# Gate and up projections by two levels of seven products, their outer weight sums made earlier and kept in DRAM

## The chip, the cores and the metric

One core of one Trainium2 chip runs the whole program. The metric is the device time of one execution in microseconds (us). Engines: TensorE (PE, its weight loads PEld), VectorE (DVE), ScalarE (ACT), GpSimd (POOL), and the queue that issues all DMAs here (SP).

## The reference

Two blocks over 512 latent tokens (and 256 context tokens in the first), width 1024, all float32: an attention and mLSTM layer, a gated linear attention layer, and then a second block with an RG-LRU branch, a gated delta branch, a merge, and a feed-forward part. The change touches the feed-forward part:

```python
    h = rmsnorm(x, ffn_norm[l])
    gu = h @ w_gate_up[l]            # 512 x 1024 by 1024 x 5632
    gt, up = jnp.split(gu, 2, axis=-1)
    x = x + (jax.nn.silu(gt) * up) @ w_down[l]
```

and, for where the new sums are made, the RG-LRU branch (12 blocks of 128 channels: a convolution over time, four 128x128 gate products, a scan forward and one backward).

## The kernel before

Data is held transposed, 128 channels by 512 tokens to a tile. One list, ORDER, holds steps such as ("gu", 3); each engine runs the steps that it knows in the order of that list (three engines take some steps of the delta stage a few places later) and waits on semaphores, so the list sets the order of work on every queue. Weights stream from DRAM into a ring of three places of 4096 columns (`ring`); SP goes through the same list, issues a place's next load once the step that frees it is passed, and waits in order for what each DMA needs.

**Gate and up.** D_FF is 2816, which makes 22 pairs j of 128 gate and 128 up columns. Pair 0 is computed plainly (32 matmul instructions of 512 columns, L1929; a float32 product is two instructions). Pairs 1 to 21 use Winograd's form of Strassen: the 2x2 blocks are the halves of the inner dimension, gate against up, and the halves of the tokens. Seven products of 4 inner tiles replace eight: 28 float32 matmuls, 56 instructions of 256 columns a pair (L1950). VectorE makes four weight sums of 512 columns a pair (`gu_s`, L3477 to L3482), adds the products up (`gu`, five additions of 256 with one operand in PSUM, L3515 to L3528), multiplies silu(gate) by up (L3490) and makes the token sums for the down projection (`down_t`, L3497 to L3503). ScalarE copies the first product and makes the silu.

**Down.** Four column blocks p of seven products of 11 inner tiles (L1977), with four weight sums of 1408 columns each by VectorE (`down_s`, L3545).

**RG-LRU stage.** `pipeline` makes 15 groups: group n holds rg_h(n-3), rg_a(n-2), rg_g(n-1), rg_u(n).

- TensorE: `rg_g` makes 16 instructions of 512 columns (L1695) and the four gates (8 instructions, L1700), which wait for the convolution of the same block; `rg_u` makes 16 (L1688).
- ScalarE: `rg_a` exp, tanh and sqrt; `rg_g` the gelu, and then four sigmoids (L2357), which wait for `rg_out` of block j-2; `rg_u` the copy of the product (L2347).
- VectorE: `rg_h`, for each of two directions a step (L3175), a product (L3179) and a scan (L3182); `rg_u` the convolution, one tensor_scalar (L3165) and three scalar_tensor_tensor (L3168).
- GpSimd: `rg_h` a sum (L3697) and a product (L3700, `rg_out`), after the second scan; `rg_a` two products (L3692).

## Time and profile before

| what | value |
|---|---|
| median of 3 runs | 3597.38 us (3597.36 to 3597.96) |
| span of the profiled execution | 3596.5 us |
| busy in the span: PE, DVE, ACT, POOL | 97%, 52%, 32%, 26% |
| chain that ended last | PE 88%, DVE 6%, ACT 3%, issue 2% |

The span runs from the first to the last instruction of one profiled execution; the median is of runs that were only timed, 0.9 us more. Busy shares are of the span. The chain that ended last is followed back from the last instruction, at each step to what released it.

### The profile page before, as it was taken

The numbers are of one execution on the slowest core, as the hardware profiler recorded it, in microseconds if no ns is written. First come the engines' busy times: TensorE is split into PE (matmuls) and PEld (weight loads), VectorE is DVE, ScalarE is ACT, GpSimd is POOL, SyncE is SP. The second block draws the span as 40 slices with busy tenths as digits, with TensorE's granted clock in tenths as the row PEclk, the third lists the DMA queues.
The fourth block names the chain that finished last, engine by engine and source line by source line (L and its number), as shares of the span: only waits on it lengthen the run. The fifth ranks groups of instructions, "written<-read, shape, count | busy, mean of one in ns | idle before, by whom it ended". The sixth has DMA issues, their size and how long they took to land.

```text
span 3596.5 us, 53959 instructions
## 1 busy us (share of the span) xinstructions
PE 3482.3 (97%) x22362; PEld 2339.3 (65%) x22362; DVE 1885.0 (52%) x3530; ACT 1160.2 (32%) x2185; POOL 921.6 (26%) x736
## 2 busy tenths in 40 slices
PE   7999999999999999999999999999999999999998
PEld 4555555655667977777777756444555545878887
DVE  3555553355445354666666653454777733554543
ACT  3443443222232022333333321775545521110100
POOL 2212221222210003555555510222545430000000
PEclk9999999999999999999999999999999999999999
DMA  5112111101012121111111111221101011221221
GB/s 228 65 74 77 51 65 53 36 36 47 25 46 106 51 85 59 41 44 48 48 48 48 54 71 59 84 76 62 48 31 48 16 74 59 106 89 76 87 81 56
DMA packets 29555, 229.78 MB, mean 64 GB/s; under 512 B 3072, under 2 KB 6784, under 8 KB 9728
## 3 DMA queue, kind: packets, MB, share of 16 engines
q1 hardware_dynamic: 29312, 226.33, 17.0%
q8 instruction: 178, 2.92, 0.3%
q14 instruction: 65, 0.53, 0.0%
HBM read 224.22 MB, written 2.10 MB: 63 GB/s over the span
## 4 chain that ended last, share of the span: by engine, by line
PE 88%; DVE 6%; ACT 3%; issue 2%; DMA 1%; POOL 1%; SPq 0%; DVEq 0%; ACTq 0%; POOLq 0%
PE bank L1295 12%; PE bank L1608 11%; PE bank L1514 7%; PE bank L1950 7%; PE bank L1602 4%; PE bank L1977 4%; PE bank L1729 3%; PE bank L1688 2%; PE bank L1868 2%; PE bank L1420 2%; PE bank L1695 2%; PE bank L1453 2%; PE bank L1242 2%; PE bank L1914 2%; PE bank L1658 1%
## 5 line engine op out<-in xcount | busy, mean ns | idle before, releaser
L1295 PE MATMUL bank<-xT,ring 128*128 128x384 f32 x896 | 323.4, 494 | 2.6 <-ACT Y L2092 2.4
L3615 POOL TENSOR_TENSOR ring<-ring 128x512 f32<-128x512 f32 x112 | 146.8, 1327 | 413.1 <-DMA ring<-in_w 411.3
L3653 POOL TENSOR_TENSOR ring<-ring 128x512 f32<-128x512 f32 x128 | 171.5, 1346 | 285.0 <-DMA ring<-in_w 284.2
L1295 PE MATMUL bank<-hT,ring 128*128 128x384 f32 x672 | 242.8, 493 | 0.0
L1608 PE MATMUL bank<-Y,ring 128*128 128x384 f32 (+1 forms) x768 | 240.7, 457 | 0.0
L1295 PEld LDWEIGHTS bank<-xT,ring 128*128 128x128 f32 x896 | 161.2, 190 | 108.3 <-issue 15.7
L3679 POOL TENSOR_TENSOR arena<-arena 128x512 f32<-128x512 f32 x112 | 184.1, 1643 | 170.8 <-PE bank L1658 155.5
L1608 PE MATMUL bank<-hT,ring 128*128 128x384 f32 (+1 forms) x576 | 184.8, 457 | 9.3 <-DVE arena L3053 8.5
L1729 PE MATMUL bank<-hT,ring 128*128 128x512 f32 x384 | 178.9, 599 | 4.7 <-ACT Y L2067 4.7
L1608 PEld LDWEIGHTS bank<-Y,ring 128*128 128x128 f32 x768 | 141.2, 190 | 64.8
L1295 PEld LDWEIGHTS bank<-hT,ring 128*128 128x128 f32 x672 | 121.4, 190 | 80.9 <-issue 16.0
L3762 POOL TENSOR_TENSOR hT<-hT,arena 128x512 f32<-128x512 f32 x3 | 5.1, 1723 | 558.6 <-ACT arena L2004 558.6
L1608 PEld LDWEIGHTS bank<-hT,ring 128*128 128x128 f32 x576 | 104.5, 190 | 58.3 <-DVE arena L3053 11.3
L3105 DVE TENSOR_TENSOR arena<-arena 128x512 f32<-128x512 f32 x112 | 95.7, 855 | 78.3 <-PE bank L1658 76.0
L3053 DVE TENSOR_TENSOR arena<-bank,arena 128x384 f32<-128x384 f32 (+1 forms) x160 | 82.1, 517 | 71.8 <-PE bank L1608 66.1
L2032 ACT ACTIVATE arena<-xT 128x512 f32<-128x512 f32 (+1 forms) x40 | 23.1, 586 | 291.0 <-DVE xT L3571 98.2
L1729 PEld LDWEIGHTS bank<-hT,ring 128*128 128x128 f32 x384 | 68.1, 190 | 73.7 <-issue 72.9
L3740 POOL TENSOR_TENSOR arena<-arena,hT 128x512 f32<-128x512 f32 x48 | 74.9, 1561 | 152.9 <-DVE arena L3290 152.9
L1950 PE MATMUL bank<-arena 128*128 128x256 f32 x504 | 112.2, 379 | 0.0
L1950 PEld LDWEIGHTS bank<-arena 128*128 128x128 f32 x504 | 95.8, 190 | 13.0
L2321 ACT ACTIVATE arena<-arena 128x512 f32<-128x512 f32 x80 | 55.1, 689 | 152.2 <-POOL arena L3679 111.2
L2820 DVE TENSOR_TENSOR arena<-arena 128x512 f32<-128x512 f32 (+3 forms) x64 | 44.5, 696 | 90.8 <-ACT arena L2206 90.8
(588 smaller groups left out, 7506.4 us busy)
## 6 DMA issues: line engine op xcount, KB each, us to landing
ring<-in_w SPq DMA_DIRECT2D x77, 1024.0 KB, 4.8
ring<-in_w SPq DMA_DIRECT2D x35, 2048.0 KB, 8.5
ring<-in_w SPq DMA_DIRECT2D x20, 1280.0 KB, 5.5
ring<-in_w SPq DMA_DIRECT2D x10, 1536.0 KB, 7.9
ring<-in_w SPq DMA_DIRECT2D x8, 1408.0 KB, 5.9
ring<-in_w SPq DMA_DIRECT2D x6, 512.0 KB, 3.5
xT<-in_xT SPq DMA_DIRECT2D x1, 3072.0 KB, 14.9
xT<-in_xT SPq DMA_DIRECT2D x4, 512.0 KB, 7.2
```

Source lines behind the costliest of these rows:

```text
L1295: ins = e.matmul(bank[spot["st", kind, n, at]][:, 0:384], left[:, k], right[:, k], start=first and k == 0, stop=k == 3, skip_group_check=True)
L1514: ins = e.matmul(o, left[:, k], right, start=first and k == 0, stop=k == m - 1, skip_group_check=True)
L1602: ins = e.matmul(m[:, sl(i)], tokens, left[:, k], start=first and i == k == 0, stop=k == 3, skip_group_check=True)
L1608: ins = e.matmul(o, left[:, k], moved, start=first and k == 0, stop=k == 3, skip_group_check=True)
L1729: ins = e.matmul(m, w[:, k, sl(i)], hT[:, k, 0:LAT], start=k == 0, stop=k == 7)
L1950: ins = e.matmul(m, l[:, k], r[:, k], start=first and k == 0, stop=k == 3, skip_group_check=True)
L1977: ins = e.matmul(m, l[:, k], r[k], start=first and k == 0, stop=k == 10, skip_group_check=True)
L3053: e.tensor_tensor(o, m, other, ALU.add).then_inc(up("gs_v", (kind, n, p)), 1)
L3105: e.tensor_tensor(o, o, gl_total(m, 0, m), ALU.mult).then_inc(up("gl_high", (j, li)), 1)
L3615: e.tensor_tensor(s[:, i], l, r, op).then_inc(up("st_s", (kind, n, i)), 1)
L3653: e.tensor_tensor(s[:, i], l, r, op).then_inc(up("gs_s", (kind, n, i)), 1)
L3679: e.tensor_tensor(o, o, gl_total(m, 1, m), ALU.mult).then_inc(up("gl_low", (j, li)), 1)
```

## The change

- The 18 pairs 4 to 21 become nine double pairs s = 2 to 10 of 256 gate and 256 up columns. Outer level: the seven products as before. Inner level: each is again seven products, over 2 inner tiles, 128 columns and 128 tokens: 98 float32 matmuls, 196 instructions of 128 columns a double pair.
- The four outer weight sums (1024 columns each) are made by GpSimd in the RG-LRU stage: 8 operations of 512 columns a double pair (`pre_s`) in each of the groups 1 to 9. SP loads 2 MB (`pre_in`) and stores 2 MB (`pre_out`) for each, two places of Y taking turns; the sums lie in a DRAM tensor. In the gate and up stage SP loads them back in four parts of 512 KB (`gq_l`). Its weight slab is 1.5 MB instead of 2 MB.
- Inner weight sums (`gq_i`): products 1 and 2 by GpSimd (4 operations of 512), products 0, 3, 4, 5, 6 by VectorE (8 of 512, 4 of 256). Inner token sums (`gq_t`) once, in places of xT that are first stored to DRAM (`x_out`) and loaded back behind the last product (`x_again`).
- Products add up in PSUM; ScalarE copies each one out, one of them also from bank to bank (`gq_c`); VectorE adds two products (`gq_v`), makes the four outer sums over 1024, 1024, 512 and 1024 columns (`gq_u`) and the product with silu (`gq_p`).
- The token sums for the down projection are made in a few wide operations in the last double pair (`down_t`); the weight sums of down block 0 go from VectorE to GpSimd, and its products are done in another order.
- The places of the last norm's squares move.

```diff
+def weight_sums(n):
+    steps = [[("pre_s", n + 1, 2 * i), ("pre_s", n + 1, 2 * i + 1)] * (0 <= n - 1 < 9) for i in range(4)]
+    return [("pre_in", n + 2)] * (n < 9), steps, [("pre_out", n + 1)] * (0 <= n - 1 < 9)
 def rg_steps():
     jobs = ([[("rg_u", j)], [("rg_g", j)], [("rg_a", j)], [("rg_h", j)]] for j in range(12))
-    return [s for n, g in enumerate(pipeline(jobs)) for s in g + RG_SIDE.get(n, [])]
+    made = []
+    for n, group in enumerate(pipeline(jobs)):
+        first, sums, last = weight_sums(n)
+        made += first
+        for i, step in enumerate(group):
+            made += [step] + sums[i] * (len(group) == 4) + [s for part in sums for s in part] * (len(group) != 4 and i == 0)
+        made += last + RG_SIDE.get(n, [])
+    return made
...
-    made = [("gu", 0), ("gu_t",), ("gu_s", 1)]
-    for j in range(1, 22):
-        made += [("gu_s", j + 1)] * (j < 21) + [("gu", j)]
-    return made + [("down_s", 0, 0), ("down_s", 0, 1), ("gu_p", 21), ("down_s", 0, 2), ("down_s", 0, 3)]
+    made = [("gu", 0), ("x_out",), ("gu_t",), ("gu_s", 1), ("gu_s", 2), ("gu", 1), ("gu_s", 3), ("gq_t", 0), ("gu", 2)]
+    made += [("gq_l", 2, 0), ("gq_l", 2, 1), ("gq_i", 2, "a"), ("gq_t", 1), ("gq_i", 2, "c"), ("gu", 3), ("gq_l", 2, 2), ("gq_l", 2, 3), ("gu_p", 3)]
+    for s in range(2, 11):
+        first, last = s == 2, s == 10
+        made += [("gq", s, 0)] + [("gq_c", s - 1, 4)] * (not first) + [("gq_c", s, 0)]
+        made += [("gq_u", s - 1)] * (not first) + [("gq_i", s, "d"), ("gq_i", s, "b"), ("gq", s, 1)] + [("gq_z", s - 1)] * (not first)
+        made += [("gq_c", s, 1)] + [("gq_l", s + 1, 0)] * (not last) + [("gq_p", s - 1)] * (not first)
+        made += [("gq", s, 2), ("gq_c", s, 2)] + [("gq_l", s + 1, 1), ("gq_i", s + 1, "a")] * (not last) + [("down_t", 0)] * last
+        made += [("gq", s, 3), ("gq_c", s, 3)] + [("gq_i", s + 1, "c")] * (not last)
+        made += [("gq", s, 4), ("gq_v", s, 0)] + [("gq_l", s + 1, 2)] * (not last) + [("down_t", 1)] * last
+        made += [("gq", s, 5), ("gq_v", s, 1)] + [("gq_l", s + 1, 3)] * (not last) + [("down_t", 2), ("down_s", 0, 2)] * last
+        made += [("gq", s, 6)]
+    return made + [("x_again",), ("gq_c", 10, 4), ("gq_u", 10), ("gq_z", 10), ("down_s", 0, 0), ("down_s", 0, 1),
+                   ("gq_p", 10), ("down_t", 3), ("down_s", 0, 3)]
...
+        GQ_OF = {0: "c", 1: "a", 2: "a", 3: "c", 4: "b", 5: "b", 6: "d"}
+        GQ_SUM = {1: 0, 2: 1, 4: 2, 5: 3}
...
+            def gq(s, i):
+                if i == 0:
+                    slab("gq", 8)
+                    spot["gu_slab", s] = open_w["gq"][1]
+                top = {0: 0, 1: 4, 2: 2, 3: 0, 4: 6, 5: 4, 6: 6}[i]
+                if i in (0, 1, 2, 4):
+                    for b in (top, top + 1):
+                        take(b, ("gq", s, i, b), {0: ("gq_c", (s, 3)), 1: ("gq_v", (s, 1)), 2: ("gq_c", (s, 2)), 4: ("gq_c", (s, 4))}[i])
+                if s == GQ_FIRST and i in (2, 4):
+                    for b, n in ((top, 256), (top + 1, 128)):
+                        ins = e.matmul(bank[b][:, 256:256 + n], ident, hT[:, 0, 0:n], start=False, stop=True, skip_group_check=True)
+                    ins.then_inc(up("gq_bits", i), 1)
+                if i == 2:
+                    q.wait_ge(*on("gq_c", (s, 0)))
+                if i == 3:
+                    q.wait_ge(*on("gq_c", (s, 0)))
+                if i == 4:
+                    q.wait_ge(*on("gq_d", s))
+                if i == 5:
+                    q.wait_ge(*on("gq_c", (s, 1)))
+                if i == 6:
+                    q.wait_ge(*on("gq_v", (s, 0)))
+                if i in (1, 2, 4, 5):
+                    q.wait_ge(*on(f"gq_l{GQ_SUM[i]}", s))
+                (x11, x12, _, x22), (s1, s2, s3, s4) = gq_blocks(gq_left(s, i)), gq_cell(i)
+                right, (t1, t2, t3, t4) = gq_right(i)
+                y11, _, y21, y22 = right[:, 0:2, 0:128], None, right[:, 2:4, 0:128], right[:, 2:4, 128:256]
+                for z, l, r in ((0, x11, y11), (4, x12, y21), (5, x22, t4), (1, s2, t2), (2, s3, t3), (3, s1, t1), (6, s4, y22)):
+                    if z == 5:
+                        q.wait_ge(*on("gq_t", ("b", 7) if i in (0, 3, 5) else ("t", 3)))
+                    if z == 1:
+                        q.wait_ge(*on(*gq_inner(s, i)))
+                    o = bank[top + (z > 3)][:, sl(z % 4)]
+                    for k in range(2):
+                        ins = e.matmul(o, l[:, k], r[:, k], start=i in (0, 1) and z in (0, 4) and k == 0, stop=k == 1,
+                                       skip_group_check=True)
+                ins.then_inc(up("gq_mm", (s, i)), 1)
+                if i == 6:
+                    give("gq", "gq_mm", (s, 6))
...
+                for n in range(7) if p else (0, 4, 2, 1, 3, 5, 6):
...
+            def gq_c(s, n):
+                q.wait_ge(*on("gq_mm", (s, {0: 0, 1: 1, 2: 2, 3: 3, 4: 6}[n])))
+                if s == GQ_FIRST and n in (0, 2):
+                    for i in (3, 4):
+                        q.wait_ge(*on("gu_u", (2 if n == 0 else 3, i)))
+                    q.wait_ge(*on("gq_bits", 2 + n))
+                if s > GQ_FIRST and n == 1:
+                    q.wait_ge(*on("gq_u", (s - 1, 3)))
+                src = {0: 0, 1: 4, 2: 2, 3: 0, 4: 6}[n]
+                lo, hi = bank[src], bank[src + 1][:, 0:384]
+                if n in (0, 2):
+                    to = 2 if n == 0 else 6
+                    e.activation(bank[to], lo, ACT.Copy)
+                    e.activation(bank[to + 1][:, 0:384], hi, ACT.Copy).then_inc(up("gq_c" if n == 0 else "gq_d", (s, 0) if n == 0 else s), 1)
+                if n:
+                    v = gq_V[:, 896 * {1: 3, 2: 1, 3: 0, 4: 2}[n]:][:, 0:896]
+                    e.activation(v[:, 0:512], lo, ACT.Copy)
+                    e.activation(v[:, 512:896], hi, ACT.Copy).then_inc(up("gq_c", (s, n)), 1)
+            def gq_silu(s):
+                q.wait_ge(*on("gq_u", (s, 3)))
+                e.activation(gq_y(s), gq_out(s, 0), ACT.Silu).then_inc(up("gq_z", s), 1)
...
+            def gq_i(s, g):
+                if g == "a":
+                    return
+                a, c, (x11, x12, x21, x22) = spot["gu_slab", s], gq_pairs[g], gq_blocks(gq_lefts(s, g))
+                q.wait_ge(*on(f"w{slot_of(a)}", a))
+                q.wait_ge(*on("x_kept"))
+                if g == "b":
+                    for n in (2, 3):
+                        q.wait_ge(*on(f"gq_l{n}", s))
+                q.wait_ge(*on(*gq_free(s, g)))
+                e.tensor_tensor(c[0], x21, x22, ALU.add).then_inc(up("gq_iv", (s, g, 0)), 1)
+                e.tensor_tensor(c[2], x11, x21, ALU.subtract).then_inc(up("gq_iv", (s, g, 2)), 1)
+                q.wait_ge(*on("gq_iv", (s, g, 0)))
+                e.tensor_tensor(c[1], c[0], x11, ALU.subtract).then_inc(up("gq_iv", (s, g, 1)), 1)
+                q.wait_ge(*on("gq_iv", (s, g, 1)))
+                e.tensor_tensor(c[3], x12, c[1], ALU.subtract).then_inc(up("gq_iv", (s, g, 3)), 1)
+            def gq_v(s, n):
+                o, top = (3, 6) if n == 0 else (1, 4)
+                q.wait_ge(*on("gq_mm", (s, 4 + n)))
+                q.wait_ge(*on("gq_c", (s, 1 + n)))
+                v = gq_V[:, 896 * o:896 * o + 896]
+                e.tensor_tensor(v[:, 0:512], bank[top], v[:, 0:512], ALU.add).then_inc(up("gq_v", (s, n, 0)), 1)
+                e.tensor_tensor(v[:, 512:896], bank[top + 1][:, 0:384], v[:, 512:896], ALU.add).then_inc(up("gq_v", (s, n)), 1)
+            def gq_u(s):
+                q.wait_ge(*on("gq_c", (s, 3)))
+                q.wait_ge(*on("gq_c", (s, 4)))
+                q.wait_ge(*on("gq_v", (s, 1)))
+                if s > GQ_FIRST:
+                    q.wait_ge(*on("gu_prod", 2 * s - 1))
+                e.tensor_tensor(gq_to(1, -1), gq_all(0, 0), gq_all(1, 3), ALU.add).then_inc(up("gq_u", (s, 0)), 1)
+                q.wait_ge(*on("gq_u", (s, 0)))
+                e.tensor_tensor(gq_to(2, -1), gq_to(1, 0), gq_all(2, 1), ALU.add).then_inc(up("gq_u", (s, 1)), 1)
+                q.wait_ge(*on("gq_u", (s, 1)))
+                e.tensor_tensor(gq_to(3), gq_to(2), gq_all(3), ALU.add).then_inc(up("gq_u", (s, 2)), 1)
+                q.wait_ge(*on("gq_u", (s, 2)))
+                e.tensor_tensor(gq_to(1, 1), gq_to(1, 1), gq_all(6, -1), ALU.add).then_inc(up("gq_u", (s, 3)), 1)
+            def gq_p(s):
+                q.wait_ge(*on("gq_z", s))
+                e.tensor_tensor(gq_y(s), gq_y(s), gq_out(s, 1), ALU.mult).then_inc(up("gu_prod", 2 * s + 1), 1)
...
+                    q.wait_ge(*on("gu_prod", 19))
+                    q.wait_ge(*on("gq_mm", (GQ_LAST, 2)))
+                    e.tensor_tensor(many(4096, 3), yf[:, 8:11, h2], yf[:, 8:11, h1], ALU.subtract).then_inc(up("down_t", (0, 1)), 1)
+                    e.tensor_tensor(many(0, 8), yf[:, 0:8, h2], yf[:, 0:8, h1], ALU.subtract).then_inc(up("down_t", (0, 0)), 1)
+                if n == 1:
+                    q.wait_ge(*on("gq_mm", (GQ_LAST, 4)))
+                    q.wait_ge(*on("down_t", (0, 0)))
+                    e.tensor_tensor(many(4864, 8), yf[:, 11:19, h2], many(0, 8), ALU.subtract).then_inc(up("down_t", (1, 0)), 1)
+                    e.tensor_tensor(many(6912, 1), yf[:, 19:20, h2], many(4096, 1), ALU.subtract).then_inc(up("down_t", (1, 1)), 1)
+                    e.tensor_tensor(yf[:, 0:9, h2], yf[:, 11:20, h2], yf[:, 0:9, h2], ALU.subtract).then_inc(up("down_t", (2, 0)), 1)
+                if n == 2:
+                    q.wait_ge(*on("gq_mm", (GQ_LAST, 5)))
+                    q.wait_ge(*on("down_t", (1, 1)))
+                    e.tensor_tensor(t4[:, 0:9], yf[:, 11:20, h1], many(4864, 9), ALU.subtract).then_inc(up("down_t", (3, 0)), 1)
+                if n == 3:
+                    q.wait_ge(*on("gu_prod", 21))
+                    e.tensor_tensor(yf[:, 9:11, h2], yf[:, 20:22, h2], yf[:, 9:11, h2], ALU.subtract).then_inc(up("down_t", (2, 2)), 1)
+                    e.tensor_tensor(many(2048, 2), yf[:, 20:22, h2], many(4352, 2), ALU.subtract).then_inc(up("down_t", (1, 2)), 1)
+                    q.wait_ge(*on("down_t", (1, 2)))
+                    e.tensor_tensor(t4[:, 9:11], yf[:, 20:22, h1], many(2048, 2), ALU.subtract).then_inc(up("down_t", (3, 2)), 1)
...
+            def pre_s(s, c):
+                half, step = c % 2, c // 2
+                s1, s2, s3, s4 = (pre_parts(s)[:, n, 2 * half:2 * half + 2] for n in range(4))
+                if c == 0:
+                    q.wait_ge(*on(f"pre_in{s % 2}", s))
+                if step:
+                    q.wait_ge(*on("pre_s", (s, c - 2)))
+                o, l, r, op = ((s1, s3, s1, ALU.add), (s3, s2, s3, ALU.subtract), (s2, s1, s2, ALU.subtract), (s4, s4, s2, ALU.subtract))[step]
+                e.tensor_tensor(o, l, r, op).then_inc(up("pre_s", (s, c)), 1)
+            def gq_i(s, g):
+                if g != "a":
+                    return
+                c, (x11, x12, x21, x22) = gq_pairs[g], gq_blocks(gq_lefts(s, g))
+                for n in (0, 1):
+                    q.wait_ge(*on(f"gq_l{n}", s))
+                q.wait_ge(*on(*gq_free(s, g)))
+                e.tensor_tensor(c[0], x21, x22, ALU.add).then_inc(up("gq_ip", (s, g, 0)), 1)
+                e.tensor_tensor(c[2], x11, x21, ALU.subtract).then_inc(up("gq_ip", (s, g, 2)), 1)
+                q.wait_ge(*on("gq_ip", (s, g, 0)))
+                e.tensor_tensor(c[1], c[0], x11, ALU.subtract).then_inc(up("gq_ip", (s, g, 1)), 1)
+                q.wait_ge(*on("gq_ip", (s, g, 1)))
+                e.tensor_tensor(c[3], x12, c[1], ALU.subtract).then_inc(up("gq_ip", (s, g, 3)), 1)
+            def down_s(p, n):
+                g_lo, g_hi, u_lo, u_hi = down_factors(p)
+                i = spot["down_slab", p]
+                l, r, op = ((u_lo, u_hi, ALU.add), (down_S[0], g_lo, ALU.subtract), (g_lo, u_lo, ALU.subtract),
+                            (g_hi, down_S[1], ALU.subtract))[n]
+                for a in (i, i + 1):
+                    q.wait_ge(*on(f"w{slot_of(a)}", a))
+                q.wait_ge(*(on("gq_mm", (GQ_LAST, 5)) if n == 2 else on("gu_prod", 21) if n == 3 else on("gq_u", (GQ_LAST, 3))))
+                if n in (1, 3):
+                    q.wait_ge(*on("down_sp", (p, n // 2)))
+                e.tensor_tensor(down_S[n], l, r, op).then_inc(up("down_sp", (p, n)), 1)
...
+            def x_out():
+                q.wait_ge(*on("h_scaled", (3, 0, 7)))
+                e.dma_start(x_kept, xT[:, 2:8, 0:LAT]).then_inc(up("x_kept", None, 16), 16)
+            def pre_in(s):
+                if s < 4:
+                    q.wait_ge(*on("sv_mm", ("oc7", 3, 0, 6)))
+                else:
+                    q.wait_ge(*on(f"pre_out{s % 2}", s - 2))
+                src = D["wg"][P * 4096 * (s - 2):P * 4096 * (s - 1)].rearrange("(p n) -> p n", p=P)
+                e.dma_start(pre_slab(s), src).then_inc(up(f"pre_in{s % 2}", s, 16), 16)
+            def pre_out(s):
+                q.wait_ge(*on("pre_s", (s, 7)))
+                e.dma_start(w_sums[s - 2], pre_slab(s)).then_inc(up(f"pre_out{s % 2}", s, 16), 16)
+            def gq_l(s, n):
+                q.wait_ge(*on(f"pre_out{s % 2}", s))
+                q.wait_ge(*(on("gq_mm", (s - 1, (1, 2, 4, 5)[n])) if s > GQ_FIRST else on("gu_mm", (2 if n < 2 else 3, 6))))
+                e.dma_start(arena_[:, 1024 * n:1024 * n + 1024], w_sums[s - 2][:, 1024 * n:1024 * n + 1024]).then_inc(up(f"gq_l{n}", s, 16), 16)
+            def x_again():
+                q.wait_ge(*on("x_kept"))
+                q.wait_ge(*on("gq_mm", (GQ_LAST, 6)))
+                e.dma_start(xT[:, 2:8, 0:LAT], x_kept).then_inc(up("x_again", None, 16), 16)
...
```

## Rows read from the trace of the kernel before

**Rows 1.** The page: busy tenths in 40 slices of the span.
```profile
PE   7999999999999999999999999999999999999998
...
POOL 2212221222210003555555510222545430000000
```

**Rows 2.** Chain that ended last, gate and up: start us, us, line, instructions.
```profile
3195.17 253.82 PE bank L1950 x1176
```

**Rows 3.** The same chain: two pieces at 128 columns, and the RG-LRU stage.
```profile
1391.92 9.38 PE bank L1602 x84
...
2279.82 6.87 PE bank L1695 x16
2286.69 3.43 PE bank L1700 x8
2290.12 6.87 PE bank L1688 x16
...
2496.83 1.13 PE bank L1770 x8
```

**Rows 4.** Timeline of GpSimd, groups 4 to 10: start us, us, [idle before <-releaser].
```profile
2288.64 1.26 POOL L3697 TENSOR_TENSOR arena<-arena 128x512 f32<-128x512 f32 x1 [12.11 <-DVE arena L3182]
...
2313.49 1.27 POOL L3697 TENSOR_TENSOR arena<-arena 128x512 f32<-128x512 f32 x1 [18.42 <-DVE arena L3182]
...
2329.84 1.26 POOL L3697 TENSOR_TENSOR arena<-arena 128x512 f32<-128x512 f32 x1 [11.28 <-DVE arena L3182]
...
2352.30 1.26 POOL L3697 TENSOR_TENSOR arena<-arena 128x512 f32<-128x512 f32 x1 [17.41 <-DVE arena L3182]
...
2354.86 2.49 POOL L3692 TENSOR_TENSOR arena<-arena 128x512 f32<-128x512 f32 x2
2367.37 1.27 POOL L3697 TENSOR_TENSOR arena<-arena 128x512 f32<-128x512 f32 x1 [10.02 <-DVE arena L3182]
...
2398.73 1.27 POOL L3697 TENSOR_TENSOR arena<-arena 128x512 f32<-128x512 f32 x1 [11.24 <-DVE arena L3182]
```

**Rows 5.** Timelines of ScalarE and VectorE, group 7.
```profile
2354.98 1.28 ACT L2357 ACT_TABLE_LOAD   x1 [7.92 <-POOL Y L3700]
...
2358.57 0.61 ACT L2347 ACTIVATE arena<-bank 128x512 f32<-128x512 f32 x1
...
2359.22 0.55 DVE L3165 TENSOR_SCALAR arena<-arena,cols 128x512 f32<-128x512 f32 x1 [7.00 <-ACT arena L2347]
2359.80 2.33 DVE L3168 SCALAR_TENSOR_TENSOR arena<-arena,cols 128x512 f32<-128x512 f32 x3
```

**Rows 6.** Timelines of VectorE and GpSimd, where both run: two stretches.
```profile
2449.32 1.66 DVE L3175 SCALAR_TENSOR_TENSOR arena<-arena 128x512 f32<-128x512 f32 x1 [2.81 <-ACT arena L2373]
2451.02 1.64 DVE L3179 TENSOR_TENSOR arena<-arena 128x512 f32<-128x512 f32 x1
...
1705.23 3.84 POOL L3653 TENSOR_TENSOR ring<-ring 128x512 f32<-128x512 f32 x3
...
1706.42 0.56 DVE L3053 TENSOR_TENSOR arena<-bank,arena 128x384 f32<-128x384 f32 x1 [1.00 <-PE bank L1608]
```

**Rows 7.** Groups by line and form: busy us, mean ns of one | idle before.
```profile
L3479 DVE TENSOR_TENSOR arena<-arena,ring 128x512 f32<-128x512 f32 x21 | 14.5, 692 | 0.7
...
L2894 DVE TENSOR_TENSOR arena<-ring 128x1024 f32<-128x1024 f32 x10 | 12.2, 1217 | 0.0
...
L3605 POOL TENSOR_TENSOR Y<-xT 128x256 f32<-128x256 f32 x8 | 6.1, 793 | 38.4 <-DMA xT<-in_xT 38.4
```

**Rows 8.** DMA issues: KB each, median us to landing.
```profile
ring<-in_w SPq DMA_DIRECT2D x35, 2048.0 KB, 8.5
...
ring<-in_w SPq DMA_DIRECT2D x6, 512.0 KB, 3.5
```

**Rows 9.** A stretch behind an idle TensorE (length, busy, PEclk, DMA), and the row before it.
```profile
549.00:552.40 3.40, 3.40 (x16) 2.04 (x17) 0.30 (x1) 0.65 (x2) 0.00 (x0) 0.62 0.00 0
...
548.73 1.11 PE L1365 MATMUL bank<-cons,arena 128*128 128x128 f32 x4 [3.16 <-ACT arena L2153]
```

172 lines of the change are left out of this document (125 added, 47 removed).

## The prediction

> **What bounds the kernel now.** I read the page's slices first, then the chain of waits, then the timelines of single engines. The slices show TensorE at nine tenths or more nearly everywhere, in the RG-LRU stage (2219 to 2460 us) and in gate and up (3195 to 3449 us) too, and GpSimd idle behind the delta stage [rows 1]. The chain shows gate and up as one piece of TensorE with no wait in it: 1176 instructions of 256 columns in 253.82 us, 0.2158 us each, so 56 x 0.2158 = 12.09 us a pair and 24.17 us for two [rows 2]. Everything that is to be gained there must shorten TensorE, and everything added must hide behind it. In the RG-LRU stage a group is 6.87 + 3.43 + 6.87 = 17.17 us of TensorE [rows 3]. But that stage has a second bound just below: a loop over three other engines. GpSimd's sum L3697 starts at 2352.30 and again at 2367.37 [rows 4], 15.07 us apart although TensorE needs 17.17: VectorE's extra work of group 6 had made the loop late, and here it catches up at its own speed. Its parts [rows 4, 5]: GpSimd's sum and product (2352.30 to 2354.9), ScalarE's table load, four sigmoids and copy (to 2359.18), VectorE's convolution (to 2362.1), then its two steps, products and scans (to 2367.3), and GpSimd again. So the stage has 2.1 us to spare in each group, and no more.
>
> **The matmuls.** 98 float32 matmuls a double pair are 196 instructions of 128 columns. The row of such a stream with a new weight each time gives 9.38 / 84 = 0.1117 us [rows 3], so 21.9 us instead of 24.17: 2.28 us less, 20.5 us less for nine. That is the gross gain. Another row at 128 columns, eight instructions with their start, has 1.13 / 8 = 0.141 [rows 3]; I take the long stream, with 2% either way (4 us).
> The Trainium skill (TensorE: Matmul & The Clock Gate, Back-to-back issue gap) speaks against this: it gives about 81 ns for a sustained pair of weight load and 128-column matmul. If a float32 instruction, which takes twice the time of its columns, paid that twice, a double pair would be 196 x 0.162 = 31.8 us by this estimate, slower than now. The row of 0.1117 us is this kernel's own, and I go by it.
>
> **The RG-LRU stage.** GpSimd gets 8 sums of 512 columns in each of groups 1 to 9, about 1.23 us each (two in 2.49 [rows 4]): 9.8 us on top of 5.1, together 14.9 of 17.17, so by busy time it fits. It is not free, because the two engines take turns when both have two operands in SBUF: VectorE's step and product took 1.66 and 1.64 us beside GpSimd's products [rows 6], where one of 512 columns takes 0.69 [rows 7]. A turn costs VectorE about 0.94 us (at most GpSimd's whole 1.27 [rows 4]). An operation with an operand in PSUM did not wait: 0.56 us for 384 columns, inside three GpSimd operations [rows 6].
> Where do the eight sums fall? Behind `rg_h` come two of them, then `rg_a`, which is done 7.5 us after the start of L3697 (2.6 + 2 x 1.23 + 2.49). VectorE's convolution starts at 6.9 (2359.22 against 2352.30). So six sums are left, and they meet the three operations of the convolution, the step, the product and the first scan: six turns, and 0.4 us for the tensor_scalar, which waits for the end of `rg_a`. All of it lies on the loop: 15.07 + 6 x 0.94 + 0.4 = 21.1 us, against TensorE's 17.17.
> By groups: 1 and 2 have no `rg_h`, and their convolutions have 3 us to spare: nothing. Group 3 starts the loop: L3697 of group 4 moves by 21.1 - 17.2 = 4. Group 4 took 24.9 us (2288.64 to 2313.49 [rows 4]), with a seventh product and a reciprocal whose waits absorb most of this: +1 stays. Group 5: 21.1 instead of 16.3, +4.8. Group 6 took 22.5, some 5 us of it extra VectorE work that also stood against a wait for TensorE and now meets some of the sums in place of the loop's operations: +1. Group 7: 21.1 instead of 15.1, +6. Groups 8 and 9: 42.2 instead of 31.4, +10.8. Together +23.6 at the start of group 10. From there the loop runs at 15.07 where TensorE's 17.17 had set the pace: 2 x 2.1 comes back, +19.4. About 1 us of it may vanish at the end, where TensorE waited for the same loop. I take **+18.5 us**. Bounds: a turn of 0.75 us gives +12, one of 1.2 us +25.
> The Trainium skill (SBUF — State Buffer, Who interferes with whom) says that whichever engine starts first holds the shared port pair for its whole instruction and the other blocks; by it a turn would cost the full 1.27 us, and the stage some 2 us a group more. The two rows beside each other show 0.94.
> TensorE will idle some 4 us in each of these groups. Behind 3.16 us of idleness the row shows a mean granted clock of 0.62 over 3.4 us [rows 9], mostly the lower level (1.2 of 2.4 GHz). Half speed for so long costs TensorE 1.7 us, and beside the loop's ScalarE part it has about 1.5 to spare: 0 to 3 us in all, kept for the range.
> SP: a load of 2 MB lands after 8.5 us [rows 8]. A store can start about 17 us after L3697; with the same 8.5 it is done at 26, the load that waits for it lands at 34 and is wanted two groups later, at 42 + 2.6. A store of 2 MB is not in the trace; up to 18 us it stays hidden. The `rg` slabs queued behind these waits are issued two groups ahead.
>
> **The steady part of gate and up.** VectorE gets, in each double pair, 8 x 0.69 + 4 x 0.42 for `gq_i`, 3 x 1.22 + 0.69 for `gq_u`, 1.22 for `gq_p` and about 2.4 for `gq_v` [rows 7] (other widths by 0.17 us and 1.03 for a thousand columns): 15.2 of 21.9 us. It fits; what counts is its order. `gq_i` "c" of the next double pair waits for product 3 (12.5 us in), runs 2.8 us, and only then comes `gq_v`, on which product 6 waits at 18.8. GpSimd's four sums wait for product 2 and the second stored part, which lands at 9.4 + 3.5 = 12.9 [rows 8]: on top of "c". Three turns (2.8 us) move the end of `gq_v` from 17.1 (it waits for product 4) to 19.5: product 6 waits 0.7 us, in seven double pairs 5 us. If the part lands 1.5 us later, 0.
>
> **Its two ends.** At the start `gq_t` (4 x 1.22 + 4 x 0.69 + 4 x 0.42 = 9.3 us) fits in the slack beside pair 2 for its first half. In pair 3 the rest of it, "c" and GpSimd's "a" meet: VectorE's additions come at 11.8 instead of 8.6 us, 3.5 us of waiting. The first double pair has extra products of 384 columns (two instructions, 0.65 us) and behind each of them two copies by ScalarE (0.6 and 0.5, and 0.2 to start) for which TensorE now waits: 2 x 2.0 = 4.0. At the end `down_t` (2048 to 2304 columns, 2.3 to 2.6 us each) stands on VectorE before `gq_u` of double pair 10, which ends 9 to 11 us behind the last product; silu 1.1, and `gq_p` in turn with GpSimd's `down_s` (1408 columns, 2.8 us from the widths 256 and 512 [rows 7]) come to 13 to 15. Down's second product wants it at 9.2. With 0.5 us behind the first product and shares of both, I take 7.7 (3 to 9). All of this was hidden before.
>
> **Sum.** Gate, up and the start of down: -20.5 + 5.0 + 3.5 + 4.0 + 7.7 = -0.3, so none (-12 to +5). RG-LRU stage +18.5. Against the profiled execution: 3596.5 + 18.5 = 3615.0, and 0.9 us around it as before: **3616 us**, 0.5% slower.
>
> **Rivals.** (A) The sums hide in GpSimd's idle time. Ten us of idleness in a group [rows 4] speak for it, rows 6 against it. Below a turn of 0.35 us (2.1 / 6) the stage costs nothing, and gate and up keep 5 us of waits at product 6 and some 3 at the ends: 3589 to 3592, faster. (B) Both cost more: a turn of 1.2 us (+25), the clock (+3), product 6 and the ends at their worst (+5): 3630. (C) DMA: with stores of 30 us SP's round trip is 17 + 30 + 8.5 = 55.5 us for two groups instead of 42.2, over six groups +40: 3656. (D) At 0.141 us an instruction a double pair is 27.6 us, nine are 31 us slower than before instead of 20.5 faster: 3667. A weight load that does not hide would do this; it is the case of the skill's rate (TensorE: Matmul & The Clock Gate).
>
> **Chances.** Forecast, 3606 to 3627: 0.62. A: 0.14, 0.11 of it faster by over 0.2% and 0.03 level. B 0.11, C 0.04, D 0.02. Between A and the forecast 0.07, 0.06 of it level. A measurement tells 0.2%, 7.2 us, from no change: faster 0.11, same 0.09, slower 0.80. The range 3600 to 3631 leaves out most of A, and C and D.
>
> **What would show it.** In groups 7 to 9 L3697 some 21 us apart and L3168 at about 1.6 us each; nine double pairs at 22 to 22.7 us, with TensorE's waits at product 6 on `gq_v` and at the start of down on `gq_p`. Wrong would be: L3697 still 15 to 17 us apart, a TensorE in the stage that waits for DMA, or double pairs at 24 us and more.

## The result, and the profile after

The changed kernel takes **3627.9 us** (median of 4 runs, 3627.3 to 3631.1), the kernel before 3597.7 (4 runs beside them, 3597.4 to 3599.4). The ratio is 1.0085, its 95% interval 1.0070 to 1.0099: slower by 0.85%. The prediction said 3616 and 3600 to 3631. The profiled execution has a span of 3625.9 us against 3596.5, so 29.4 us are to be found.

I went through the span from its start and set the starts of the same TensorE instructions against each other. The lead of the kernel before grows in four places: 1.2 us in the first 40 us of the program, where nothing was changed; 23.1 us in the RG-LRU stage; 4.0 in the delta stage behind it; 1.0 in gate, up and down together. That is 29.3. The first of the four belongs to the execution and not to the change: up to the RG-LRU stage all kernels below do the same work as the kernel before, and their profiles lie between 6.0 us ahead of it and 2.4 us behind.

The page's first lines of the changed kernel:

```profile
PE 3479.7 (96%) x23126; PEld 2350.7 (65%) x23126; DVE 1996.6 (55%) x3512; ACT 1198.8 (33%) x2248; POOL 1100.4 (30%) x848
...
POOL 2212121222210014555555412762444420002210
...
L4045 POOL TENSOR_TENSOR Y<-Y 128x512 f32<-128x512 f32 x72 | 107.6, 1526 | 0.0
```

The last row is the 72 outer sums: 1.53 us each instead of the 1.25 that they take where VectorE is idle (two in 2.49 below). GpSimd's two slices that lie wholly in the stage show seven and six tenths, two before [rows 1]: it is far from full, as forecast, and yet the stage is longer. GpSimd's timeline there, the sum in `rg_h` (L3970, L3697 before), groups 4 to 11; this answers to [rows 4]:

```profile
2294.26 1.26 POOL L3970 TENSOR_TENSOR arena<-arena 128x512 f32<-128x512 f32 x1 [5.18 <-DVE arena L3375]
2317.05 1.27 POOL L3970 TENSOR_TENSOR arena<-arena 128x512 f32<-128x512 f32 x1 [4.36 <-DVE arena L3375]
2338.08 1.26 POOL L3970 TENSOR_TENSOR arena<-arena 128x512 f32<-128x512 f32 x1 [3.73 <-DVE arena L3375]
2364.22 1.27 POOL L3970 TENSOR_TENSOR arena<-arena 128x512 f32<-128x512 f32 x1 [9.12 <-DVE arena L3375]
2385.21 1.26 POOL L3970 TENSOR_TENSOR arena<-arena 128x512 f32<-128x512 f32 x1 [3.73 <-DVE arena L3375]
2406.25 1.26 POOL L3970 TENSOR_TENSOR arena<-arena 128x512 f32<-128x512 f32 x1 [3.73 <-DVE arena L3375]
2427.26 1.27 POOL L3970 TENSOR_TENSOR arena<-arena 128x512 f32<-128x512 f32 x1 [3.73 <-DVE arena L3375]
2442.33 1.26 POOL L3970 TENSOR_TENSOR arena<-arena 128x512 f32<-128x512 f32 x1 [10.01 <-DVE arena L3375]
```

Four of the steps from one such sum to the next are 21.0 us long (21.03, 20.99, 21.04, 21.01), and GpSimd waits 3.73 us for VectorE's scan in each. One round of the loop, first VectorE, then GpSimd:

```profile
2392.14 0.88 DVE L3358 TENSOR_SCALAR arena<-arena,cols 128x512 f32<-128x512 f32 x1 [7.01 <-ACT arena L2516]
2393.05 4.99 DVE L3361 SCALAR_TENSOR_TENSOR arena<-arena,cols 128x512 f32<-128x512 f32 x3
2397.97 1.76 DVE L3368 SCALAR_TENSOR_TENSOR arena<-arena 128x512 f32<-128x512 f32 x1
2399.76 1.64 DVE L3372 TENSOR_TENSOR arena<-arena 128x512 f32<-128x512 f32 x1
2401.43 2.17 DVE L3375 TENSOR_TENSOR_SCAN arena<-arena 128x512 f32<-128x512 f32 x1
2403.53 0.66 DVE L3368 SCALAR_TENSOR_TENSOR arena<-arena 128x512 f32<-128x512 f32 x1
```

```profile
2387.78 2.49 POOL L4045 TENSOR_TENSOR Y<-Y 128x512 f32<-128x512 f32 x2
2390.23 2.50 POOL L3965 TENSOR_TENSOR arena<-arena 128x512 f32<-128x512 f32 x2
2392.68 9.84 POOL L4045 TENSOR_TENSOR Y<-Y 128x512 f32<-128x512 f32 x6
```

The convolution's three operations take 4.99 us where the row of before has 2.33 [rows 5]. The step takes 1.76, the product 1.64 and the scan 2.17; their twins a little later, with GpSimd idle, take 0.66, 0.69 and 1.22. These are six turns (times that VectorE waits for a GpSimd operation to end) beside the six sums, 5.7 us together.

TensorE's waits from gate and up to the end of down, in us, times and the longest:

```profile
PE bank L2146 <- ACT arena L2757: 8.9, 1, 8.9
PE bank L2117 <- DVE arena L3730: 3.5, 5, 0.7
...
PE bank L2117 <- ACT bank L2719: 2.2, 2, 1.1
```

And the chain that ended last, where down begins (start us, us, what):

```profile
3474.89 1.24 DVE arena L3741
...
3476.88 1.24 DVE arena L3745
...
3478.13 1.06 ACT Y L2727
...
3479.21 1.28 ACT L2184
...
3480.50 0.39 ACT arena L2757
...
3480.94 130.34 PE bank L2146 x594
```

The eight double pairs behind the first take 21.89 us (three) or 22.85 (five, those with a wait at product 6), the first 25.95.

### The profile page after: what moved, and what is told of

It reads as the page before. It is cut to its first block, busy times and chain, and to the rows that moved or that the text cites. A ratio compares the mean times of both kernels' runs of the same rounds, so it can differ in the third digit from the quotient of the medians.

```text
span 3625.9 us, 55742 instructions
## 1 busy us (share of the span) xinstructions
PE 3479.7 (96%) x23126; PEld 2350.7 (65%) x23126; DVE 1996.6 (55%) x3512; ACT 1198.8 (33%) x2248; POOL 1100.4 (30%) x848
## 3 DMA queue, kind: packets, MB, share of 16 engines
q1 hardware_dynamic: 38656, 281.38, 21.1%
## 4 chain that ended last, share of the span: by engine, by line
PE 81%; DVE 10%; ACT 4%; issue 3%; POOL 1%; DMA 1%; SPq 0%; DVEq 0%; ACTq 0%; POOLq 0%
PE bank L1423 12%; PE bank L1736 11%; PE bank L1642 7%; PE bank L2117 4%; PE bank L1730 4%; PE bank L2146 4%; PE bank L1857 3%; PE bank L1996 2%; PE bank L1548 2%; PE bank L1581 2%; PE bank L1370 2%; PE bank L2042 2%; PE bank L1786 1%; PE bank L1509 1%; PE bank L1994 1%
## 5 line engine op out<-in xcount | busy, mean ns | idle before, releaser
L4054 POOL TENSOR_TENSOR hT<-arena 128x512 f32<-128x512 f32 x9 | 13.6, 1514 | 327.0 <-DMA arena<-w_sums 327.0
L4045 POOL TENSOR_TENSOR Y<-Y 128x512 f32<-128x512 f32 x72 | 107.6, 1526 | 0.0
L3916 POOL TENSOR_TENSOR arena<-arena,cons 128x128 f32<-128x128 f32 x48 | 31.0, 645 | 219.7 <-DVE arena L3013 219.7
```

What stands on the lines that cost most here:

```text
L4045: e.tensor_tensor(o, l, r, op).then_inc(up("pre_s", (s, c)), 1)
```

## The experiments

All are edits of the changed kernel; its 3628 us is the mark. Each was timed against the kernel before on its chip: 3598.6, 3599.1 and 3599.3 us for the three sets.

**e1_no_sums: no outer sums, all their transfers.**

```
-                  "dn_yd": dn_yd, "pre_s": pre_s, "gq_i": gq_i, "down_s": down_s, "nh": nh}
+                  "dn_yd": dn_yd, "gq_i": gq_i, "down_s": down_s, "nh": nh}
...
             def pre_out(s):
-                q.wait_ge(*on("pre_s", (s, 7)))
+                q.wait_ge(*on(f"pre_in{s % 2}", s))
```

The first two lines are GpSimd's table of steps. The store now waits for its load and not for the last sum.

> The changed kernel without GpSimd's 72 outer sums in the RG-LRU stage: the factors are loaded and stored unsummed, every load and store keeps its place (the products of gate and up then read the factors themselves, so this part of the computation is changed). Turns between VectorE and GpSimd (my theory): the stage's 23 us go, L3697's counterpart is again 15 to 17 us apart in groups 7 to 9, and if the 4 us more in the delta stage are the clock's answer to the idle time they go too: 3628 - 27 = 3601 us, so 0 to 5 us over the kernel before. Rival, the 36 MB of loads and stores or SP's waits delay the stage: at least 15 of the 23 us stay, 3616 us or more. Rival for the delta stage, its 4 us have a cause of their own: 3605 us.

Measured: 3599.4 us, ratio 1.0005 (0.9996 to 1.0014). L3970 is 15.07 us apart in groups 7 and 8, and every interval between two L3970 is within 0.02 us of the one before. So the 36 MB of transfers cost nothing in this order, and all 23 us are the sums'. Of the delta stage's 4.0 us 2.2 stay in this profile, by the starts of the same instructions. Windows of the delta stage (length, busy times, then the granted clock), the kernel before and this one:

```profile
2522.50:2527.50 5.00, 3.84 (x99) 2.31 (x100) 3.15 (x5) 3.10 (x6) 2.70 (x2) 0.70 0.02 3
```

```profile
2532.00:2542.00 10.00, 8.87 (x118) 3.95 (x122) 5.64 (x7) 5.38 (x11) 4.45 (x4) 0.66 0.01 2
```

Both have one dip of the clock to a mean of 0.7, that is, partly at 1.2 instead of 2.4 GHz; before it lies over 5 us, here over 10, some 10 us later and in other work. That is 1.5 against 3.4 us. The rival, a cause apart from the sums, is neither shown nor refuted by this. What the delta stage costs is 4.1 us again in e3_c_behind_v and e4_end, whose programs up to there are that of the changed kernel. But it is 0.0 in e6_half and e10_vector, which keep sums in the stage before, and 4.0 in e7_u_first_but_5 and 1.0 in e8_all, two kernels whose programs do not differ up to there. So it changes from one execution to the next as well.

**e6_half: four of the eight sums in a group.**

```
                 if c == 0:
                     q.wait_ge(*on(f"pre_in{s % 2}", s))
+                if c >= 4:
+                    return
...
-                q.wait_ge(*on("pre_s", (s, 7)))
+                q.wait_ge(*on("pre_s", (s, 3)))
```

The second part lets the store wait for the fourth sum, now the last.

> The changed kernel with only the first four of a group's eight outer sums, 36 instead of 72 (two behind rg_h, two behind rg_a; the other four are left out, which changes this part of the computation). Theory: only the two behind rg_a still meet the loop, 15.07 + 2 x 0.94 + 0.4 = 17.35 us against TensorE's 17.17, so the stage costs 0 to 3 us and the time is 3602 us (3599 to 3606). Rival, the cost goes with the number of sums, half of the 28 us that leaving all of them out gave back: 3614 us.

Measured: 3604.0 us (1.0012, 1.0003 to 1.0021). L3970 is 17.16 and 17.17 us apart in groups 7 to 9, TensorE's own pace (I had 17.35), and TensorE waits once in the stage, 3.6 us. Taking half of the sums away takes away nearly the whole cost: it goes by what is left over TensorE's 17.17 us, not by their number.

**e2_u_first: the same sums, the loop cut.**

```
+        named = {step[0]: step for step in group}
+        group = [named[name] for name in ("rg_h", "rg_a", "rg_u", "rg_g") if name in named]
```

> The changed kernel with rg_u(n) ahead of rg_g(n-1) in every group of the RG-LRU stage, on all engines: ScalarE's copy for the next convolution no longer stands behind the four sigmoids that wait for GpSimd's rg_h, so the loop over three engines is cut, while each turn stays. Theory, turns cost because they lie on this loop: what is left is throughput, VectorE 9 operations with turns of 0.94 us (about 15 us) and GpSimd 12 operations of 1.24 us plus its own turns of about 0.4 us (about 18.5 us a group instead of 21): of the 23 us about 9 stay, 3614 us (3605 to 3619). Rival, the pace of 21 us is set by the turns alone wherever they stand: 3628 us.

Measured: 3613.5 us (1.0043, 1.0028 to 1.0058), so the loop and not the turns as such made most of the cost. The sum in `rg_h` is still 19.9 us apart in groups 7 to 10; this is now GpSimd's throughput, its operations stand back to back, and one operation of GpSimd with one of VectorE takes 1.67 us. But TensorE no longer follows it: behind group 7 its groups take 17.2 us each. What it waits for in the stage is something else:

```profile
PE bank L1818 <- DMA ring<-in_w: 6.0, 2, 5.5
```

The long one is at `rg_u` of group 6. The ring has three places, and with the slab `ba` in it the slab of group 6 takes the place of group 4's. In this order `rg_g(4)` frees that directly ahead of `rg_u(6)`: TensorE finished the one, the load was issued at 2324.3 us, and TensorE went on at 2329.8. Its first instruction starts 6.12 us behind the one ahead of it, where 0.43 is usual: 5.7 us more. The next seven steps are 0.69 to 1.01 us long, most of them 0.85, where 0.43 is usual: 3.0 us more, at the lower level of the clock (a mean of 0.54 over these 6.3 us). The stage still costs 9.5 us in this profile, and nearly all of it is this one slab.

**e7_u_first_but_5: the same with the old order in group 5.**

```
+        if n != 5:
+            group = [named[name] for name in ("rg_h", "rg_a", "rg_u", "rg_g") if name in named]
```

> As the kernel with rg_u first, but with the old order in group 5 alone. Theory: the 5.8 us of TensorE's waiting that were left there (at L1818, for the load of the slab of group 5, whose place in the ring rg_g of group 3 gave free only before the ba product) and some 2.7 us of half clock behind it go: 3613.5 - 8.5 = 3605 us (3602 to 3608), 0 to 3 us of the stage's 23 left. Rival, the old order brings the loop of 21 us back in groups 5 and 6: 3610 to 3614 us.

Measured: 3613.0 us (1.0038, 1.0024 to 1.0051). My theory gave 8 us more than came. It had named the wrong slab (group 5's for group 6's), and what it gained was lost again, though not to the loop, as the rival had it. TensorE's waits in the stage and SP's issues there:

```profile
PE bank L1819 <- DMA ring<-in_w: 6.7, 2, 4.9
```

The wait at group 6 shrank to 1.8 us, and one of 4.9 us came up at group 10, with 16 instructions in 9.58 us instead of 7.03 behind it; the stage costs 9.7 us, as much as in e2. The same wait stands in the profile of e8_all, whose stage has the same order (e7 issues the same three transfers at 2379.89, 2386.19 and 2386.56 us). SP's timeline in e8_all (L4147 stores sums, L4143 loads factors, L4106 loads weights) shows why:

```profile
2380.55 0.33 SPq L4147 DMA_DIRECT2D w_sums<-Y  x1
2386.85 0.33 SPq L4143 DMA_DIRECT2D Y<-in_wg  x1
2387.22 0.43 SPq L4106 DMA_DIRECT2D ring<-in_w  x1
```

```profile
2398.09 9.40 PE L1819 MATMUL bank<-hT,ring 128*128 128x512 f32 x16 [4.84 <-DMA ring<-in_w]
```

GpSimd, at 19.9 us a group, is more than a group behind TensorE by now. SP waits for its last sum of group 7 (2380.55), then for the store to land before the next factors may come (2386.85), and only behind these two the load of weights is issued, whose place `rg_g(7)` had freed at 2376.1 (2372.48 and 3.60 us). TensorE wanted it at 2393.2. Rival C had such a wait in SP's queue, but from stores of 30 us; here the stores are quick and GpSimd's sums are late. It shows only once the loop no longer holds TensorE back as well.

**e5_copies: one operand instead of two.**

```
-                e.tensor_tensor(o, l, r, op).then_inc(up("pre_s", (s, c)), 1)
+                e.tensor_copy(o, l).then_inc(up("pre_s", (s, c)), 1)
```

> The changed kernel with each of GpSimd's 72 outer sums in the RG-LRU stage replaced by a copy of its left operand, 512 columns as before, so one operand in SBUF instead of two (the stored parts are then not sums: this part of the computation is changed). Theory, turns are taken between operations with two operands in SBUF: the stage's 23 us go as they do without the sums, 3601 us (3598 to 3606). Rival, any operation of GpSimd that reads SBUF keeps VectorE's two-operand ones waiting: what stays is by the length of the copies, 3615 to 3628 us.

Measured: 3602.5 us (1.0012, 1.0003 to 1.0021). The time is what my theory gave, and its reason is false. VectorE, then GpSimd:

```profile
2353.84 0.63 DVE L3358 TENSOR_SCALAR arena<-arena,cols 128x512 f32<-128x512 f32 x1 [7.01 <-ACT arena L2516]
2354.51 3.00 DVE L3361 SCALAR_TENSOR_TENSOR arena<-arena,cols 128x512 f32<-128x512 f32 x3
2357.43 1.09 DVE L3368 SCALAR_TENSOR_TENSOR arena<-arena 128x512 f32<-128x512 f32 x1
2358.55 0.69 DVE L3372 TENSOR_TENSOR arena<-arena 128x512 f32<-128x512 f32 x1
```

```profile
2349.47 1.16 POOL L4045 COPY Y<-Y 128x512 f32<-128x512 f32 x2
...
2353.03 4.96 POOL L4045 COPY Y<-Y 128x512 f32<-128x512 f32 x6
```

The copies take turns with VectorE too. They are only short: 0.56 us apart undisturbed, so a turn costs VectorE some 0.3 us instead of 0.95, and the loop's 16.24 us fit into TensorE's 17.17. The rival that every read of SBUF by GpSimd counts is right in the mechanism, and I had put its price too high. That the time fell into my range is therefore luck.

**e3_c_behind_v: the inner sums "c" behind the additions for product 6.**

```
-        ... ("gq_c", s, 3)] + [("gq_i", s + 1, "c")] * (not last)
-        ... ("gq_v", s, 0)] + [("gq_l", s + 1, 2)] * (not last)
+        ... ("gq_c", s, 3)]
+        ... ("gq_v", s, 0)] + [("gq_i", s + 1, "c"), ("gq_l", s + 1, 2)] * (not last)
```

> The changed kernel with VectorE's inner sums c of the next double pair moved behind the additions gq_v for product 6. Theory: TensorE's wait of 0.7 us at product 6 (0.97 us with its restart, in five double pairs) is the turns of c with GpSimd's inner sums, and it goes: 4.9 us less, 3623 us. Rival: c, now some 6 us later, is itself late for the first product of the next double pair: a wait moves there and the time stays at 3626 to 3630 us.

Measured: 3623.4 us (1.0072, 1.0057 to 1.0087). The row of five waits at product 6 is gone from the list and no other takes its place. The span is 4.6 us shorter.

**e4_end: another order at the start of down.**

```
-        made += [("gq", s, 5), ("gq_v", s, 1)] + [("gq_l", s + 1, 3)] * (not last) + [("down_t", 2), ("down_s", 0, 2)] * last
+        made += [("gq", s, 5), ("gq_v", s, 1)] + [("gq_l", s + 1, 3)] * (not last) + [("down_s", 0, 2)] * last
...
-    return made + [("x_again",), ("gq_c", 10, 4), ("gq_u", 10), ("gq_z", 10), ("down_s", 0, 0), ("down_s", 0, 1),
-                   ("gq_p", 10), ("down_t", 3), ("down_s", 0, 3)]
+    return made + [("x_again",), ("gq_c", 10, 4), ("gq_u", 10), ("down_c",), ("gq_z", 10), ("gq_p", 10), ("down_s", 0, 0), ("down_s", 0, 1),
+                   ("down_t", 4), ("down_t", 3), ("down_t", 2), ("down_t", 5), ("down_s", 0, 3)]
...
```

`down_c` is ScalarE's copy of down's first product. `down_t` 4 and 5 are what was the last addition of `down_t` 1 and of `down_t` 3. GpSimd's first two sums wait for `gq_p`. These are three moves in one, and what each of them gives is not separated.

> The changed kernel with another order at the start of down: ScalarE copies the first product ahead of the last silu, the two additions for down of 2304 columns stand behind gq_p instead of ahead of gq_u, and GpSimd's first two sums for down wait for gq_p instead of taking turns with it. Theory: TensorE's 8.9 us of idleness behind down's first product are that copy and these turns; the last gq_u starts at about 3468 instead of 3473 us and gq_p ends at about 3475 instead of 3482 us, behind which the second product has nine of its eleven parts to do anyway: idle time 0 to 2 us, 3620 us (3618 to 3622). Rival: the additions behind gq_p are late for the third and fourth product in their turn and give half of it back: 3624 us.

Measured: 3619.4 us (1.0057, 1.0036 to 1.0077), 10.0 us less than the changed kernel in the span. TensorE's waits in down:

```profile
PE bank L2146 <- POOL arena L4077: 1.5, 1, 1.5
...
PE bank L2146 <- ACT arena L2761: 0.5, 1, 0.5
PE bank L2146 <- DVE Y L3770: 0.3, 1, 0.3
```

2.3 us instead of 8.9. The size is less sure than these rows. Three of the four runs took 3617.6 to 3623.2 us at a mean granted clock of 0.990 or 0.991, and the fourth 3609.1 at 0.994. And the 10.0 us of the span hold 2.9 that the edit does not explain: this profile has two waits at product 6 instead of five, though that part is unchanged.

**e8_all: e7, e3 and e4 together.**

> The three edits together: rg_u first except in group 5, the inner sums c behind gq_v, and the other order at the start of down. Theory, they are independent: against the changed kernel's 3628 us, 14.4 + 8.5 from the RG-LRU stage, 4.5 from the steady part, 8.5 from the start of down (7 of them seen as idle time), 3592 us (3588 to 3597), faster than both kernels. Rival, the gains overlap or the clock's dips come back: 3597 to 3602, level with the kernel before.

Measured: 3601.1 us (3593 to 3603, ratio 1.0000, 0.9991 to 1.0009): level with the kernel before, and my estimate was 9 us too low. Some 8 us of it are the gain that e7 did not bring, which I had counted on before knowing it.

**e10_vector: the outer sums by VectorE, nothing else changed.** `pre_s` moves from GpSimd's table of steps to VectorE's, word for word, with its semaphore.

> The changed kernel with the eight outer sums of a group made by VectorE (0.69 us each) instead of GpSimd (1.24), in the same places of the order. Theory: six of them fall into the 6.9 us in which VectorE waits for GpSimd's rg_h and ScalarE's copy anyway, with some four turns against rg_h and rg_a, and two stand behind the convolution on the loop: 15.07 + 1.2 (two turns that GpSimd's rg_h waits) + 0.3 + 1.4 = 18.0 us a group against 17.17 of TensorE; of the stage's 23 us about 4 are left and the 4 of the delta stage go: 3604 us (3599 to 3609). Rival, VectorE is the longest member of the loop, so all of its 5.5 us lie on it: 20.6 us a group, 3622 us.

Measured: 3604.6 us (1.0013, 1.0004 to 1.0022). The sum in `rg_h` is 17.06 us apart in groups 7 to 9 (I had 18.0). VectorE's timeline of one group:

```profile
2352.11 7.96 DVE L3694 TENSOR_TENSOR Y<-Y 128x512 f32<-128x512 f32 x6
2359.99 0.54 DVE L3358 TENSOR_SCALAR arena<-arena,cols 128x512 f32<-128x512 f32 x1
2360.56 2.33 DVE L3361 SCALAR_TENSOR_TENSOR arena<-arena,cols 128x512 f32<-128x512 f32 x3
2362.81 1.29 DVE L3694 TENSOR_TENSOR Y<-Y 128x512 f32<-128x512 f32 x2
```

Six sums fill the gap in which VectorE waited for ScalarE's copy, with all turns inside it, the convolution is back at 2.33 us, and only 1.29 us lie on the loop. TensorE waits once in the stage, 2.0 us.

**e11_old_order_vector: e10, e3 and e4 together.**

> As the kernel with VectorE's outer sums, with the inner sums c behind gq_v and the other order at the start of down as well, rg_g and rg_u in their old order. Theory, the three are independent: 3604 - 4.5 - 8.5 = 3591 us (3587 to 3597). Rival, the one of the kernel before: 3599 us.

Measured: 3591.4 us, ratio 0.9978 (0.9970 to 0.9987): faster than the kernel before and the changed kernel.

**e9_all_vector: e8 with the outer sums by VectorE.**

> As the kernel with the three edits together (rg_u first except in group 5), with the outer sums made by VectorE. Theory: a group then holds 4 x 1.24 us of GpSimd's and 15 x 0.43 + 2 x 0.95 us of VectorE's time in turns, 13.3 us instead of 19.9, so GpSimd no longer falls behind, the stores are issued in time and the slab that TensorE waited 4.8 us for (behind a store in SP's queue) comes in time; the 2 us of waiting at the slab of group 6 stay: 3592 us (3588 to 3597), the same as or slightly above the kernel with the old order. Rival, the waits for slabs come from the new order and not from late stores: 3598 us or more.

Measured: 3588.7 us, ratio 0.9971 (0.9959 to 0.9982). It is 0.3% faster than the kernel before and 39 us faster than the changed kernel. Its interval overlaps that of e11_old_order_vector, so the runs do not show that the new order still gains anything once VectorE makes the sums. TensorE's only wait in the stage, and the stage's window (PE, PEld, DVE, ACT and POOL busy):

```profile
PE bank L1819 <- DMA ring<-in_w: 1.7, 1, 1.7
```

```profile
2220.00:2460.00 240.00, 236.59 (x553) 104.99 (x554) 186.63 (x219) 159.67 (x210) 75.89 (x54) 0.99 0.61 229
```

The wait of 4.8 us at group 10 is gone with GpSimd's lateness, as its theory says. VectorE's busy time includes its waits for turns.

## Why the prediction came out right, and where its terms were off

The measured 3627.9 us lie in the stated range, but 11.9 us above its point and 0.9 above the 3606 to 3627 that had got 0.62, nearer to rival B's 3630. The direction and the mechanism of the largest term were forecast. All four parts of the difference came out above the forecast and none below, and two of them, 5.2 us, were not in the sum; that the time still fell in the range owes something to its width.

**The matmuls: right.** A double pair without waits is 21.89 us for 196 instructions, 0.1117 each, the value of [rows 3] to the last digit. The Trainium skill's sustained rate (TensorE: Matmul & The Clock Gate, Back-to-back issue gap), taken twice for a float32 instruction, would have given 31.8; no double pair shows it. Rival D is out.

**The RG-LRU stage: mechanism right, size 4.6 us too low (18.5 against 23.1).** The loop, the six sums that it meets and its 21.1 us stand in the trace as 21.0; e1 shows that the sums make all of it, e6 that four of eight fit under 17.17, e2 that the cost hangs on the loop. A turn cost 0.95 us (0.94 taken). Interval by interval of L3970, changed kernel less before, with my value in brackets: +4.4 (4), -2.1 (-3), +4.7 (4.8), +3.7 (1), +5.9 (6), +6.0 and +4.7 (10.8 for both), -2.1 and -2.1 (-4.2), end 0 (-0.9). The term that was most off is **"+1" for group 6**, 2.7 of the 4.6 us; the rest is mainly 0.4 at group 3, 0.9 at group 4 and the 0.9 that did not vanish at the end. I let its additional VectorE work of 5 us absorb turns twice: once as slack against TensorE, once as other work that meets the sums. Its own rows show 5.8 us of turns, the whole set, between the start of the convolution and L3970 (19.2 us instead of 13.4), and only 2.1 us of waiting for TensorE were there to absorb them:

```profile
2338.86 0.55 DVE L3165 TENSOR_SCALAR arena<-arena,cols 128x512 f32<-128x512 f32 x1 [9.11 <-ACT arena L2347]
```

```profile
2345.01 0.86 DVE L3358 TENSOR_SCALAR arena<-arena,cols 128x512 f32<-128x512 f32 x1 [7.01 <-ACT arena L2516]
```

The first is the kernel before, the second the changed kernel. Work on the same engine is no slack: it moves the turn to another operation of the same chain.

**SP: right here.** e1 keeps every transfer and costs nothing, and a store landed after 7.5 us, not 30, so rival C is out. e7 and e8 show where this ends.

**The clock: kept out of the sum, and it is in the result.** The windows have 0.63 over the 4.6 us behind the stage's last idle time and 0.69 over 11 us in the delta stage:

```profile
2484.40:2489.00 4.60, 4.60 (x7) 2.00 (x8) 0.40 (x1) 3.98 (x7) 1.27 (x1) 0.63 0.00 0
...
2557.00:2568.00 11.00, 8.70 (x107) 3.91 (x106) 5.65 (x7) 6.53 (x13) 4.66 (x4) 0.69 0.01 1
```

The clock took 1.7 and 3.4 us there; less the 1.5 us of the dip that the kernel before has, this is most of the delta stage's 4.0. It is not a steady cost of the sums. As told at e1, the same stretch costs 0.0 to 4.1 us in the profiles, and 4.0 or 1.0 with one and the same program. At the start of the RG-LRU stage the kernel before has such a dip itself: its first 16 instructions (L1688) take 8.80 us, their counterpart in e1 7.11. What sets the place and the length of these dips is open.

**Steady gate and up: right in the mechanism, and in the size by two errors that cancel.** Product 6 waits 0.70 us for `gq_v`, with 0.97 in all for the double pair; I had 0.7. It does so in five double pairs, not seven, so 4.9 us against 5.0. e3 shows the cause: the turns of "c" with GpSimd's "a" in front of `gq_v`. Which double pairs wait is a matter of 0.1 us. In the five that do, GpSimd's first sum of "a" starts 13.17 to 13.34 us into the double pair, ahead of VectorE's third of "c"; in two that do not it starts at 13.42 and 13.44, behind it, and `gq_v` starts at 17.35 instead of 18.43. So the number of waits is not a constant: with this part unchanged it is four in e1, six in e2 and two in e4. The prediction had put this escape at 1.5 us.

**The first double pair: right, +4.1** (4.0). **Pair 3: +1.4 instead of +3.5**; TensorE waited 1.2 us for it once.

**The end: +11.2 instead of +7.7, and not for the reason given.** I had the second product wait for `gq_p`. The chain shows ScalarE's copy of the first product (L2757), for which the second waits before it starts: it stands in ScalarE's queue behind the last silu and a table load of 1.28 us, and the silu behind VectorE's late `gq_u`. The product that waits needs `gq_p` only for its last two parts. I had costed the copy at 0.5 us of its own duration and had not asked what is queued ahead of it. Of the 11.2, 8.9 are idle time; the rest is a slow start behind it, 6.87 us for 22 instructions that take 22 x 0.2158 = 4.75 at the rate of [rows 2]:

```profile
3480.94 6.87 PE L2146 MATMUL bank<-Y,ring 128*128 128x256 f32 x22 [8.91 <-ACT arena L2757]
```

The mean granted clock of these 6.7 us is 0.71, so it is at its lower level for part of them; I had no term for that. VectorE's addition of 2304 columns beside GpSimd's first sum for down took 5.52 us where the next, alone, takes 2.54.

```profile
3464.67 5.52 DVE L3765 TENSOR_TENSOR Y<-Y 128x2304 f32<-128x2304 f32 x1
...
3471.17 2.54 DVE L3769 TENSOR_TENSOR Y<-Y,arena 128x2304 f32<-128x2304 f32 x1
```

**The sum.** Gate, up and down came to +1.0 (forecast -0.3): nine double pairs -11.7, start 1.4, end 11.2. The expected gain of 20.5 us was real and was spent again inside its own stage, 4.1 + 4.9 + 1.4 + 11.2. The parts come to 29.3 us where the forecast's come to 18.2: 4.6 more in the RG-LRU stage, 4.0 in the delta stage, 1.3 from gate to down, 1.2 at the start of the program. Rival B has the size that came (3630), but by a turn of 1.2 us, and the turn is 0.95. Rival A is out by the time itself, and by e1: the sums do not hide on GpSimd. They hide on VectorE (e10).

## What to carry to other kernels

Work put on an idle engine costs what it takes from the loop that engine is in: list the other engines' operations that run in the same stretch, count a turn for each, and compare the loop's length (not the busy times) with the bound. The idle time worth filling is the one in which the whole loop waits for someone else, here VectorE's 7 us ahead of the convolution, even if that engine is the busier one. Where a phase ends, ask of every small operation what stands ahead of it in its own queue: TensorE waited 8.9 us for a copy of 0.4 us.
